# Splitting the gather of the next expert pair's tokens into two parts between the gate and up products of a mixture-of-experts layer

## The chip, the cores and the metric

The kernel runs on one core of one Trainium2 chip. The metric is the device time of one launch in microseconds (us). The kernel before takes 1908.6 us, the median of three runs (1907.25, 1908.6 and 1911.63).

## What is computed

An encoder of two layers over 256 tokens of width 2048, all in float32. Each layer has a mixer (latent attention, dilated attention and an mLSTM, joined by `w_out`) and then a hierarchical mixture of 16 experts of which each token takes two. Only the experts matter for this change. From the reference:

```
def hier_moe(x, wg, bg, we, be, w_gate, w_up, w_down):
    ...
    w = jax.nn.softmax(top_v, axis=-1) * p_grp[..., None]
    eid = grp[..., None] * EXPERTS_PER_GROUP + top_i
    comb = jnp.sum(jax.nn.one_hot(eid, N_EXPERTS, dtype=f32) * w[..., None], axis=-2)
    h = jax.nn.silu(jnp.einsum('bsd,edf->bsef', x, w_gate)) * jnp.einsum('bsd,edf->bsef', x, w_up)
    h = h * comb[..., None].astype(h.dtype)
    return jnp.einsum('bsef,efd->bsd', h, w_down)
```

D_MODEL is 2048 and D_EXPERT 512, so one expert has three weight matrices of 4 MB, and the 16 experts of a layer have 201 MB.

## The kernel before

**The experts in rounds.** The kernel works on two experts at a time, in `NE // 2` = 8 rounds of a layer. An expert has room for CAP = 64 tokens, so a pair fills the 128 columns of the TensorE array: expert 0 of the pair on rows 0 to 63 of the output and expert 1 on rows 64 to 127. The products of the two run side by side on the two halves of the array (form 128*64 in the trace). TensorE executes each float32 matmul of the program as two instructions in the trace.

**One round on TensorE** (lines 1139 to 1175), for the pair i:

- `expert("g0", i)`, `expert("u0", i)`, `expert("g1", i)`, `expert("u1", i)`: gate and up projection, each in two halves of 256 columns. One such call is 32 matmuls of the program (64 in the trace) and reads two loads of weights, one of each expert.
- `turn_h(0, i)` and `turn_h(1, i)` (line 1117): transposes of the gated product, after DVE has multiplied the two halves (line 1816).
- `gather(i + 1)` (lines 1086 to 1096): it picks the tokens of the *next* pair out of `xtok` (in `PR`) by a product with a one-hot matrix `Gm` (in `v_mla`), 4 PSUM banks gx0 to gx3 of 8 matmuls each (32 of the program, 64 in the trace, form 128*128). ScalarE copies the four banks to `XG` (line 2133) once u1 of the present pair is done, since the present pair reads `XG` until then.
- `scatter(i - 1, ...)`: the last pair's result goes back to the tokens; DVE adds it to `X` (line 1787).
- the transposes of line 1159 (weights of the scatter), and then four products dy0 to dy3 with the down projection. They read the loads dn0 (two) and dn1 (two).

**DVE in a round** (lines 1811 to 1834): the product of line 1816 for half 0, the one-hot matrices of the next pair (`tokens_of_pair(i + 1)`, line 1774, stage `gm`) and of the scatter (`gw`), the copy of the transposed half, the same for half 1 with the additions to `X`, and at the round's end the copies of dy1 and dy3 (line 1834).

**The weights.** SyncE's queue (`load`, lines 606 to 610) issues the loads in the order of the list `EXPERT`: for each round g0, g0, u0, u0, g1, g1, u1, u1, dn0, dn0, dn1, dn1. Each is 2 MB. They go round nine places in SBUF (six of `ring`, and `BIAS`, `XN` and `PR`, which are free in this stage). A load waits until the product that read the load nine places before it in the list is done:

```
        def empty(name, l):
...
            if at > 0:
                return ready(LAST_READER.get(before, before), l)
```

Nine of a layer's 96 loads are therefore issued before the first product (they are loads 1 to 9 below), and loads 10 and 11 wait for g0 of round 0, loads 12 and 13 for u0, 14 and 15 for g1, 16 and 17 for u1, 18 and 19 for dy1 of round 0, and so on in the same order through the layer. SyncE works through its waits in order.

**The order of the work** is written out by hand; each engine waits on semaphores: `psum_full` (a bank is written), `psum_free` (a bank is read), `slot_full` (a load has landed) and one for each stage such as `gm`.

Of the kernel before, what the change touches and what calls it, by code (L numbers as in the profile page):

```python
# [52 lines left out]
NE = NG * EPG  # L53
# [312 lines left out]
def build(nc, a, consts, onehot, lncount, out):  # L366
    with ExitStack() as ctx:
# [146 lines left out]
        def after(name, l, j=0, i=None, stride=0):  # L514

            s, n = stages[name]
            return s, l * n + (j + 1) + (0 if i is None else i * stride)
# [9 lines left out]
        def bank(name):  # L527
            return ps[:, BANKS.where(name), :]

        def ready(name, l=0):  # L530

            return psum_full[BANKS.where(name)], BANKS.before(name, l) + 1

        def freed(name, l=0):

            return psum_free[BANKS.where(name)], BANKS.before(name, l)

        def copied(name, l=0):

            return psum_free[BANKS.where(name)], BANKS.before(name, l) + 1  # L540

        def made(name):
            return psum_full[BANKS.where(name)], 1
# [4 lines left out]
        def slot(name):  # L548
            s = SLOTS.where(name)
            return ring[:, s, :] if s < NSLOT else spare[s]  # L550
# [17 lines left out]
        def loaded(name, l):  # L568
            s = SLOTS.where(name)
            return slot_full[s], 16 * (SLOTS.before(name, l) + 1)  # L570
# [131 lines left out]
        def _(pe):  # L702
            def mm(o, lhsT, rhs, start=True, stop=True):
                return pe.matmul(o, lhsT, rhs, start=start, stop=stop, skip_group_check=True)  # L704
# [175 lines left out]
            for l in range(DEPTH):  # L880
# [202 lines left out]
                mm(bank("count")[:, 0:NE], ones[:, :], picked[:, 0, 0:NE], True, False)  # L1083
                mm(bank("count")[:, 0:NE], ones[:, :], picked[:, 1, 0:NE], False, True).then_inc(*made("count"))

                def gather(i):

                    pe.wait_ge(*after("gm", l, i))
                    for n in range(4):
                        name = f"gx{n}_{i}"  # L1090
                        pe.wait_ge(*freed(name, l))
                        for k in range(4):
                            d = (4 * n + k) * P
                            for t in range(NT):
                                last = mm(bank(name)[:, k * 2 * CAP:(k + 1) * 2 * CAP], xtok[:, t, d:d + P], Gm[:, t, :], t == 0, t == NT - 1)
                        last.then_inc(*made(name))

                def expert(n, i):

                    name = f"{n}_{i}"  # L1100
                    w = [slot(f"{n}{j}_{i}").rearrange("p (k c) -> p k c", k=KT) for j in range(2)]
                    for j in range(2):
                        pe.wait_ge(*loaded(f"{n}{j}_{i}", l))
                    pe.wait_ge(*freed(name, l))
                    for k in range(KT):
                        for j in range(2):
                            own_rows = slice(j * CAP, (j + 1) * CAP)
                            last = mm(bank(name)[own_rows, 0:CH], XG[:, k, own_rows], w[j][:, k, :], k == 0, k == KT - 1)
                    last.then_inc(*made(name))

                def turn_h(half, i):

                    name = f"ht{half}_{i}"
                    pe.wait_ge(*copied(f"u{half}_{i}", l))
                    pe.wait_ge(*freed(name, l))
                    for q in range(2):
                        last = pe.transpose(bank(name)[:, q * 2 * CAP:(q + 1) * 2 * CAP], gated[:, (2 * half + q) * P:(2 * half + q + 1) * P], ident)  # L1117
                    last.then_inc(*made(name))

                def scatter(i, ks):  # L1120

                    for k in ks:
                        name = f"sc{k}_{i}"
                        pe.wait_ge(*freed(name, l))
                        for q in range(2):
                            last = mm(bank(name)[:, q * S:(q + 1) * S], Y[:, (2 * k + q) * P:(2 * k + q + 1) * P], Sw)
                        last.then_inc(*made(name))

                def written(i):
                    pe.wait_ge(*copied(f"sw_{i}", l))  # L1130
                    for n in range(4):
                        pe.wait_ge(*copied(f"dy{n}_{i}", l))
# [6 lines left out]
                for i in range(NE // 2):  # L1139
                    for n in range(4):  # L1140
                        pe.wait_ge(*copied(f"gx{n}_{i}", l))
                    expert("g0", i)
                    expert("u0", i)
                    expert("g1", i)
                    turn_h(0, i)
                    if i + 1 < NE // 2:
                        gather(i + 1)
                    expert("u1", i)
                    if i >= 1:
                        written(i - 1)  # L1150
                        scatter(i - 1, range(KT // 4))
                    turn_h(1, i)
                    if i >= 1:
                        scatter(i - 1, range(KT // 4, KT // 2))

                    pe.wait_ge(*freed(f"sw_{i}", l))
                    pe.wait_ge(*after("gw", l, i))
                    for t in range(NT):
                        last = pe.transpose(bank(f"sw_{i}")[0:2 * CAP, t * P:(t + 1) * P], Gw[:, t, :], ident)  # L1159
                    last.then_inc(*made(f"sw_{i}"))  # L1160

                    for half in range(2):
                        pe.wait_ge(*copied(f"ht{half}_{i}", l))
                    for half in range(2):
                        w = [slot(f"dn{half}{j}_{i}").rearrange("p (k c) -> p k c", k=4) for j in range(2)]
                        for j in range(2):
                            pe.wait_ge(*loaded(f"dn{half}{j}_{i}", l))
                        for q in range(2):
                            name = f"dy{2 * half + q}_{i}"
                            pe.wait_ge(*freed(name, l))  # L1170
                            for k in range(4):
                                for j in range(2):
                                    own_rows = slice(j * CAP, (j + 1) * CAP)
                                    last = mm(bank(name)[own_rows, :], hs[:, k, own_rows], w[j][:, k, q * 512:(q + 1) * 512], k == 0, k == 3)
                            last.then_inc(*made(name))
# [3 lines left out]
                with pe.If(due > 0):  # L1179

                    i = NE // 2 - 1
# [87 lines left out]
        def _(dve):  # L1269
# [121 lines left out]
            for l in range(DEPTH):  # L1391
# [385 lines left out]
                def tokens_of_pair(i):  # L1777
                    for j in range(2):
                        ins = one_hot(Gm[:, :, j * CAP:(j + 1) * CAP], 2 * i + j, seen)
                    ins.then_inc(*signal("gm"))  # L1780
# [28 lines left out]
                for n in (1, 3):  # L1809
                    gathered(f"gx{n}_0", n, l)  # L1810
                for i in range(NE // 2):
                    for half in range(2):

                        dve.wait_ge(*copied(f"g{half}_{i}", l))
                        dve.wait_ge(*ready(f"u{half}_{i}", l))
                        dve.tensor_tensor(gated[:, half * CH:(half + 1) * CH], sgs[:, half * CH:(half + 1) * CH],  # L1816
                                          bank(f"u{half}_{i}")[0:2 * CAP, 0:CH], ALU.mult).then_inc(*read(f"u{half}_{i}"))
                        if half == 0:
                            if i + 1 < NE // 2:
                                tokens_of_pair(i + 1)  # L1820
                            for j in range(2):
                                ins = one_hot(Gw[:, :, j * CAP:(j + 1) * CAP], 2 * i + j, comb)
                            ins.then_inc(*signal("gw"))
                        elif i >= 1:
                            add_moe(i - 1, range(KT // 4))
                        dve.wait_ge(*ready(f"ht{half}_{i}", l))
                        dve.tensor_copy(hs[:, 2 * half:2 * half + 2, :].rearrange("p k n -> p (k n)"), bank(f"ht{half}_{i}")[:, 0:4 * CAP]).then_inc(*read(f"ht{half}_{i}"))  # L1827
                    if i >= 1:
                        add_moe(i - 1, range(KT // 4, KT // 2))
                    dve.wait_ge(*ready(f"sw_{i}", l))  # L1830
                    dve.tensor_copy(Sw, bank(f"sw_{i}")[0:2 * CAP, 0:S]).then_inc(*read(f"sw_{i}"))
                    for n in (1, 3):
                        dve.wait_ge(*ready(f"dy{n}_{i}", l))
                        dve.tensor_copy(Y[:, n * 512:(n + 1) * 512], bank(f"dy{n}_{i}")[0:2 * CAP, :]).then_inc(*read(f"dy{n}_{i}"))  # L1834
# [388 lines left out]
```

## Time and profile before

| | |
|---|---|
| median of three runs | 1908.6 us |
| the profiled execution, its own time | 1908.6 us |
| its span, first to last instruction | 1906.8 us |
| PE busy | 1858.8 us (97%) |
| PE weight loads | 1403.1 us (74%) |
| DVE, ACT busy | 624.6 us (33%), 312.2 us (16%) |
| granted TensorE clock, mean | 0.997 of full |
| DMA moved | 544.68 MB, mean 286 GB/s |

The page cuts the span into 40 equal slices of 47.7 us. The experts of layer 0 take about 500 to 952 us, those of layer 1 about 1444 to 1903 us. A row of the chain of waits gives the start of a piece, its length and what ran there; "issue" is time in which the engine waited for nothing that the profile shows. A load's issue is the instruction on SyncE's queue, and "to landing" is the time from there until the last of its 16 parts is in SBUF.

### The profile page before, as it was taken

How to read it: one execution, taken by the hardware profiler on the slowest of the kernel's cores; microseconds unless marked ns; L12 is line 12 of the kernel's file. 1: busy time of each engine (PE TensorE's matmuls, PEld its weight loads, DVE VectorE, ACT ScalarE, POOL GpSimd, SP SyncE). 2: the span in 40 equal slices, each digit the busy share in tenths (PEclk: the TensorE clock that was granted, in tenths of full speed). 3: DMA queues.
4: the chain of work that ended last, by engine and by line, in shares of the span. 5: the costliest groups of instructions: out<-in, count | busy, mean ns of one | idle time of the engine just before them, and what ended most of it. 6: DMA issues, size and time to landing. Idle time of an engine off the chain costs nothing.

```text
span 1906.8 us, 26494 instructions
## 1 busy us (share of the span) xinstructions
PE 1858.8 (97%) x11558; PEld 1403.1 (74%) x11558; DVE 624.6 (33%) x1361; ACT 312.2 (16%) x845; POOL 7.4 (0%) x15
## 2 busy tenths in 40 slices
PE   7999999999999999999999999999999999999998
PEld 7788888788866666656597888877878656666655
DVE  2467664222201221121235675622221121221112
ACT  2122222211211111011021131321111111111010
POOL 0000000000000000000000000000000000000000
PEclk9999999999999999999999999999999999999999
DMA  8342344253699999999694243351647999999995
GB/s 347 141 172 109 156 175 177 96 210 143 273 425 427 426 427 426 428 427 427 287 375 158 113 177 116 150 226 45 246 150 310 425 427 428 427 426 427 428 428 247
DMA packets 40551, 544.68 MB, mean 286 GB/s; under 512 B 4744, under 2 KB 4872, under 8 KB 7792
## 3 DMA queue, kind: packets, MB, share of 16 engines
q1 hardware_dynamic: 38448, 531.46, 67.4%
q0 software_dynamic: 1728, 11.42, 1.5%
q8 instruction: 96, 1.57, 0.3%
q14 instruction: 23, 0.19, 0.0%
q10 hardware_dynamic: 256, 0.04, 0.0%
HBM read 538.69 MB, written 4.22 MB: 285 GB/s over the span
## 4 chain that ended last, share of the span: by engine, by line
PE 95%; DVE 2%; issue 1%; ACT 1%; DMA 1%; SPq 0%; DVEq 0%
PE ps L704 92%; PE ps L758 1%; DMA ring<-in_w_lat 1%; PE ps L1117 1%; ACT prob L1923 0%; PE ps L774 0%; DVE ring L1341 0%; DVE ring L1499 0%; DVE ring L1493 0%; DVE ring L1495 0%; PE ps L766 0%; DVE PR L1580 0%; DVE ss_d L1545 0%; PE ps L1035 0%; PE ps L1159 0%
## 5 line engine op out<-in xcount | busy, mean ns | idle before, releaser
L704 PE MATMUL ps<-ring,scr 128*64 128x256 f32 (+2 forms) x3520 | 559.5, 426 | 7.8 <-issue 7.8
L704 PEld LDWEIGHTS ps<-ring,scr 128*64 128x64 f32 (+1 forms) x3520 | 319.0, 139 | 203.3 <-issue 114.4
L704 PE MATMUL ps<-ring,XN 128*128 128x256 f32 (+2 forms) x1184 | 245.1, 364 | 12.5 <-DMA ring<-in_w_lat 12.5
L704 PEld LDWEIGHTS ps<-ring,XN 128*128 128x128 f32 x1184 | 212.7, 192 | 33.5 <-issue 14.4
L704 PE MATMUL ps<-ring,X 128*128 128x256 f32 x896 | 201.4, 379 | 3.6 <-ACT PR L2002 3.6
L704 PEld LDWEIGHTS ps<-ring,X 128*128 128x128 f32 x896 | 169.8, 190 | 27.3 <-ACT PR L2002 4.4
L704 PE MATMUL ps<-XN,ring 128*128 128x256 f32 x768 | 170.4, 381 | 0.9 <-DVE prob L1303 0.9
L704 PEld LDWEIGHTS ps<-XN,ring 128*128 128x128 f32 x768 | 144.7, 190 | 26.6 <-issue 7.7
L704 PE MATMUL ps<-BIAS,scr 128*64 128x256 f32 (+1 forms) x608 | 157.6, 417 | 6.7 <-issue 6.7
L704 PE MATMUL ps<-PR,scr 128*64 128x256 f32 (+2 forms) x576 | 158.3, 430 | 0.7 <-DVE scr L1827 0.7
L1816 DVE TENSOR_TENSOR v_mla<-scr,ps 128x256 f32<-128x256 f32 x32 | 13.5, 421 | 428.7 <-PE ps L704 428.7
L704 PE MATMUL ps<-XN,scr 128*64 128x256 f32 (+1 forms) x576 | 141.6, 403 | 1.9 <-issue 1.8
L704 PE MATMUL ps<-PR,ring 128*128 128x256 f32 x640 | 142.9, 383 | 0.0
L704 PEld LDWEIGHTS ps<-PR,ring 128*128 128x128 f32 x640 | 121.8, 192 | 19.0 <-issue 2.7
L704 PE MATMUL ps<-PR,prob 128*128 128x256 f32 x512 | 117.0, 382 | 2.3 <-DVE prob L1834 2.3
L704 PE MATMUL ps<-v_mla,PR 128*128 128x128 f32 x1024 | 117.0, 275 | 0.0
L704 PEld LDWEIGHTS ps<-v_mla,PR 128*128 128x128 f32 x1024 | 115.6, 192 | 0.0
L704 PEld LDWEIGHTS ps<-PR,prob 128*128 128x128 f32 x512 | 94.9, 190 | 21.0 <-issue 9.4
L704 PEld LDWEIGHTS ps<-BIAS,scr 128*64 128x64 f32 x608 | 82.9, 138 | 33.3 <-issue 9.7
L704 PEld LDWEIGHTS ps<-PR,scr 128*64 128x64 f32 (+1 forms) x576 | 81.2, 146 | 34.6 <-issue 24.9
L704 PEld LDWEIGHTS ps<-XN,scr 128*64 128x64 f32 x576 | 78.2, 137 | 31.0 <-issue 21.0
L2133 ACT ACTIVATE scr<-ps,par 128x128 f32<-128x128 f32 x240 | 64.0, 413 | 214.4 <-PE ps L704 214.4
(250 smaller groups left out, 1250.6 us busy)
## 6 DMA issues: line engine op xcount, KB each, us to landing
ring<-in_moe_w_up SPq DMA_DIRECT2D x44, 2048.0 KB, 22.9
ring<-in_moe_w_down SPq DMA_DIRECT2D x44, 2048.0 KB, 26.8
ring<-in_moe_w_gate SPq DMA_DIRECT2D x42, 2048.0 KB, 25.0
ring<-in_w_main SPq DMA_DIRECT2D x36, 2048.0 KB, 9.0
ring<-in_w_out_a SPq DMA_DIRECT2D x10, 2048.0 KB, 10.1
PR<-in_moe_w_down SPq DMA_DIRECT2D x10, 2048.0 KB, 24.5
XN<-in_moe_w_gate SPq DMA_DIRECT2D x10, 2048.0 KB, 28.6
BIAS<-in_moe_w_up SPq DMA_DIRECT2D x10, 2048.0 KB, 23.9
```

The source lines that it names most:

```text
L704: return pe.matmul(o, lhsT, rhs, start=start, stop=stop, skip_group_check=True)
L758: last = pe.transpose(bank(name)[:, (kt * NT + t) * P:(kt * NT + t + 1) * P], prob[:, u % 2, j, t, kt * P:(kt + 1) * P], ident)
L1117: last = pe.transpose(bank(name)[:, q * 2 * CAP:(q + 1) * 2 * CAP], gated[:, (2 * half + q) * P:(2 * half + q + 1) * P], ident)
L1816: dve.tensor_tensor(gated[:, half * CH:(half + 1) * CH], sgs[:, half * CH:(half + 1) * CH], bank(f"u{half}_{i}")[0:2 * CAP, 0:CH], ALU.mul ...
L2133: ins = act.activation(XG[:, 4 * n + k, :], bank(name)[:, k * 2 * CAP:(k + 1) * 2 * CAP], ACT.Copy, scale=pcol(l, R_FFN + 4 * n + k))
```

## The change

`gather` takes a list of banks and is called twice in a round, after g0 and after u0, instead of once after `turn_h(0)`. DVE makes the one-hot matrix of the next pair at the start of the round:

```
@@ -1083,10 +1083,10 @@
-                def gather(i):
+                def gather(i, ns=range(4)):
 
                     pe.wait_ge(*after("gm", l, i))
-                    for n in range(4):
+                    for n in ns:
                         name = f"gx{n}_{i}"
                         pe.wait_ge(*freed(name, l))
@@ -1140,11 +1140,13 @@
                     expert("g0", i)
+                    if i + 1 < NE // 2:
+                        gather(i + 1, (0, 1))
                     expert("u0", i)
+                    if i + 1 < NE // 2:
+                        gather(i + 1, (2, 3))
                     expert("g1", i)
                     turn_h(0, i)
-                    if i + 1 < NE // 2:
-                        gather(i + 1)
                     expert("u1", i)
@@ -1809,6 +1811,10 @@
                 for i in range(NE // 2):
+                    if i + 1 < NE // 2:
+                        for n in range(4):
+                            dve.wait_ge(*ready(f"gx{n}_{i}", l))
+                        tokens_of_pair(i + 1)
                     for half in range(2):
@@ -1816,8 +1822,6 @@
                         if half == 0:
-                            if i + 1 < NE // 2:
-                                tokens_of_pair(i + 1)
                             for j in range(2):
```

The number of instructions and of loads stays the same, and so do the banks and the places of the loads.

On PE, round 0 of layer 0, from the last product of g0 to the first of u1, before (`ring,scr` are products of weights, `v_mla,PR` is the gather, L1117 turn_h(0)):

```order
L704 MATMUL ps<-BIAS,scr 64x256
L704 MATMUL ps<-ring,scr 64x256 x65
L1117 MATMUL ps<-K,v_mla 128x128 x2
L704 MATMUL ps<-v_mla,PR 128x128 x32
L704 MATMUL ps<-ring,scr 64x256
```

And the same place with the change:

```order
L704 MATMUL ps<-BIAS,scr 64x256
L704 MATMUL ps<-ring,scr 64x256
L704 MATMUL ps<-v_mla,PR 128x128 x16
L704 MATMUL ps<-ring,scr 64x256 x32
L704 MATMUL ps<-v_mla,PR 128x128 x16
L704 MATMUL ps<-ring,scr 64x256 x32
L1117 MATMUL ps<-K,v_mla 128x128 x2
L704 MATMUL ps<-ring,scr 64x256
```

Half of the gather now stands between g0 and u0 and half between u0 and g1; the transposes of line 1117 are followed by u1 at once.

On DVE, rounds 0 and 1 of layer 0, before (L1774 are the one-hot matrices, eight in a row: four for the next pair, four for the scatter):

```order
L1816 TENSOR_TENSOR v_mla<-scr,ps 128x256 [waits psum_full1,psum_free0]
L1774 TENSOR_SCALAR v_mla<-PR 128x64 x8
L1827 COPY scr<-ps 128x256 [waits psum_full0]
L1816 TENSOR_TENSOR v_mla<-scr,ps 128x256 [waits psum_full3,psum_free2]
L1827 COPY scr<-ps 128x256 [waits psum_full3]
```

With the change (its lines 1776, 1822 and 1831 are lines 1774, 1816 and 1827 of before):

```order
L1776 TENSOR_SCALAR v_mla<-PR 128x64 [waits psum_full6,psum_full7,psum_full5,psum_full4]
L1776 TENSOR_SCALAR v_mla<-PR 128x64 x3
L1822 TENSOR_TENSOR v_mla<-scr,ps 128x256 [waits psum_full1,psum_free0]
L1776 TENSOR_SCALAR v_mla<-PR 128x64 x4
L1831 COPY scr<-ps 128x256 [waits psum_full0]
```

The four for the next pair now stand ahead of the product of half 0 and behind a wait for the four gather banks of the present pair.

## Rows read from the trace of the kernel before

**Rows 1.** The page: DMA share in 40 slices, and what moved
```profile
DMA  8342344253699999999694243351647999999995
GB/s 347 141 172 109 156 175 177 96 210 143 273 425 427 426 427 426 428 427 427 287 375 158 113 177 116 150 226 45 246 150 310 425 427 428 427 426 427 428 428 247
```

**Rows 2.** Chain that ended last, in time order: start, length (us), what
```profile
707.23 0.22 PE ps L1159 x2
...
763.95 0.22 PE ps L1159 x2
...
821.70 0.22 PE ps L1159 x2
...
850.23 2.67 issue
...
883.61 0.22 PE ps L1159 x2
...
919.12 2.29 issue
921.41 12.46 PE ps L704 x80
...
1863.64 2.29 issue
```

**Rows 3.** One issue on SyncE's queue, and its landing: load 92
```profile
L610 SPq DMA_DIRECT2D ring<-in_moe_w_up x1: 328/328/328, 897.8 to 897.8; - x1
DMA to landing us min/median/max: 23.6/23.6/23.6
```

**Rows 4.** Stretches: PE, PEld, DVE, ACT, POOL busy, PEclk, DMA share, GB/s
```profile
500.00:508.00 8.00, 7.95 (x74) 6.43 (x76) 0.00 (x0) 0.38 (x1) 0.00 (x0) 1.00 0.00 0
...
540.00:921.00 381.00, 375.15 (x2779) 245.22 (x2774) 66.76 (x146) 39.23 (x124) 0.00 (x0) 1.00 1.01 427
```

**Rows 5.** Loads 10, 12, 14, 16 and 24: issue on SyncE's queue, landing
```profile
L610 SPq DMA_DIRECT2D BIAS<-in_moe_w_down x1: 328/328/328, 507.2 to 507.2; - x1
DMA to landing us min/median/max: 8.0/8.0/8.0
...
L610 SPq DMA_DIRECT2D ring<-in_moe_w_down x1: 327/327/327, 514.1 to 514.1; - x1
DMA to landing us min/median/max: 11.2/11.2/11.2
...
L610 SPq DMA_DIRECT2D ring<-in_moe_w_gate x1: 327/327/327, 521.0 to 521.0; - x1
DMA to landing us min/median/max: 14.4/14.4/14.4
...
L610 SPq DMA_DIRECT2D ring<-in_moe_w_up x1: 328/328/328, 535.6 to 535.6; - x1
DMA to landing us min/median/max: 10.8/10.8/10.8
...
L610 SPq DMA_DIRECT2D ring<-in_moe_w_down x1: 328/328/328, 565.0 to 565.0; - x1
DMA to landing us min/median/max: 20.5/20.5/20.5
```

**Rows 6.** PE in order of time, round 0: start, length (us), instructions
```profile
520.92 0.44 PE L1117 MATMUL ps<-K,v_mla 128*128 128x128 f32 x2
521.20 7.31 PE L704 MATMUL ps<-v_mla,PR 128*128 128x128 f32 x64
...
527.78 0.72 PE L704 MATMUL ps<-v_mla,PR 128*128 128x128 f32 x5
528.44 0.43 PE L704 MATMUL ps<-ring,scr 128*64 128x256 f32 x1
```

**Rows 7.** DVE in order of time, rounds 0 and 1
```profile
489.30 0.98 DVE L1774 TENSOR_SCALAR v_mla<-PR 128x64 f32<-128x64 f32 x4
...
551.21 0.69 DVE L1834 COPY prob<-ps 128x512 f32<-128x512 f32 x1 [6.17 <-PE ps L704]
```

## The prediction

> **What bounds the kernel now.** I read the page's slices first. From slice 12 to 19 (about 520 to 905 us) and from slice 32 to 39 the 16 DMA engines are full and move 425 to 428 GB/s [rows 1]: the stretches of the experts' weights. PE looks full there too, so the question is which of the two sets the end of a layer. For that I read the chain in order of time. The transposes of line 1159 close each round. From round 3 to round 4 they are 763.95 - 707.23 = 56.72 us apart, with no idle piece on PE. A round reads 12 loads of 2.097 MB. At 427 GB/s [rows 4] one takes 4.91 us, so a round of loads takes 58.9 us. PE is faster than its weights by 2.2 us a round, eats up its lead of nine loads, and then waits: round 5 takes 821.70 - 763.95 = 57.75 us, round 6 takes 61.91 us, and in round 7 PE idles 2.29 us before u1 [rows 2]. That last idle time ends at 921.41 us. Load 92, the second one of u1 in round 7, is issued at 897.8 and lands 23.6 us later, at 921.4 [rows 3]. From there on the work of layer 0 is fixed. Layer 1 does the same: it idles 2.29 us from 1863.64 [rows 2]. So each layer ends a fixed time after its load 92, and the step to cost is what the change does to the line of loads. PE has room of 1.03 + 5.19 + 2.29 = 8.5 us a layer.
>
> The line has no hole. Load 10 lands at 507.2 + 8.0 = 515.2 [rows 5] and load 92 at 921.4: 82 loads in 406.2 us, 4.95 us each. It begins when g0 of round 0 is done, since the DMA engines moved nothing from 500 to 508 us [rows 4]. The change can move load 92 only by moving that start or by making a hole.
>
> **The parts of the change.**
>
> *One-hot matrices earlier on DVE.* In round 0 the four for pair 1 now follow DVE's copies of the first gather, which PE waits for anyway. They take 0.98 us [rows 7] while g0 runs for 6.9 us. In a later round they follow the copy of dy3, which ends at 551.9, so they are done by 552.9 to 553.1. PE wants them after g0 of round 1, about 558. Their new wait for the banks of the present pair is long met, and behind it only the product of half 0 is queued, which waits for u0. Cost 0. If this cover were gone, PE would stand still at the first half of the gather for at most the 0.98 us.
>
> *Banks.* The first half needs gx0 and gx1 free, which are the banks of dy0 and dy1 of the round before. Their copies end within a microsecond of dy1 and dy3, one product before the gather asks. Cost 0. ScalarE's copies to `XG` still wait for u1. Cost 0.
>
> *More changes of form on PE.* Three products of 64 columns (6.92 us each) run from 500.05, and the transposes start at 520.92 [rows 6], so leaving this form costs about 0.1 us. Inside the gather the instructions follow at (527.78 - 521.20) / 59 = 0.1115 us. The last five would end their turns at 528.34, and u1 starts at 528.44 [rows 6]: 0.1 us for coming back. Before, transposes and gather share one such visit. Now there are three visits, two more of 0.2 us: 0.4 us a round, 2.8 us over the seven rounds with a gather. That fits in the room of 8.5 us of the same layer, because the idle time before load 92 only shrinks. Cost 0 while the weights are the bound.
>
> The Trainium skill, "TensorEngine Tiling (Array Packing)", section Key Properties, speaks against the change: changing the tiling mode drains TensorE. It gives no figure. The trace agrees that a change of form costs something, 0.1 us each way here. By the rule with a large drain the sum would be that of the third rival below.
>
> *Places in SBUF free later, in round 0.* This is the term that counts. Half a gather is 32 x 0.1115 + 0.2 = 3.8 us. g0 stays where it is. u0 is done 3.8 us later and g1 7.6 us later. u1 is late by the 0.4 us alone. So load 10 is issued at 507.2 as before, load 12 at 514.1 + 3.8 = 517.9, load 14 at 521.0 + 7.5 = 528.5 and load 16 at 536.0 instead of 535.6 [rows 5]. Loads 10 and 11 are 9.8 us of data. They land at 515.2 and 520.1 to 520.4. A load that finds the engines empty lands 8.0 us after its issue (load 10), of which 4.9 us is data, so the issue must be 3.1 us ahead of the end of the line. At 517.9 it is only some 2.4 us ahead. Two estimates follow.
>
> - Low: load 12 at 517.9 + 8.0 = 525.9 instead of 525.3, load 14 at 528.5 + 8.0 = 536.5 instead of 535.4, so 1.1 us late. Then load 16 may get some back. Before, it is issued at 535.6 with only load 15 in front (about 535.4 + 4.9 = 540.3) and lands at 546.4, 6.1 us after it instead of 4.9. Now it would be issued 5.4 us ahead of load 15's end (541.4) and could land at 546.3. Nothing is lost. If the 6.1 us steps don't appear at loads 12 and 14 at all, up to 1.2 us is won.
> - High: each load that comes with too little in front of it costs a step of 6.1 us, as load 16 did. Load 12 then lands at 526.5 (1.2 us late), load 14 at 537.5 (2.1 us late), and load 16 keeps its own 6.1 us step: 2.1 us late.
>
> I take the high row for loads 12 and 14, being the nearest (load 16 had 4.7 us in front when it was issued, these have less), and give load 16 its step back, since it now has more in front: 2.1 - 1.2 = 0.9, rounded to 1.0 us a layer. Ends: 1.2 us won, 2.1 us lost.
>
> In round 1 the same delay hurts nothing. Load 24 is issued at 565.0 and lands 20.5 us later [rows 5], so 15.6 us of loads are in front of it when it is issued. It can come 3.8 us later, and its successor 7.6 us later. After that PE is faster than the loads and the line in front grows (23.6 us to landing at load 92).
>
> *Idle time of late rounds.* The halves now stand where PE waits for weights, such as the 2.67 us at 850.23 [rows 2], and fill it. PE then reaches u1 of round 6 sooner and waits there or in round 7. Cost 0, gain 0, since load 92 doesn't move.
>
> **Sum.** 2 layers x 1.0 = 2.0 us on the profiled execution's 1908.6 us (its span 1906.8), which is also the median of the runs: 1910.6 us. A difference of 0.2% (3.8 us) is about what a measurement of this kernel can tell from no change, so I forecast no difference that can be told.
>
> **Rivals.**
>
> 1. *The line of loads really runs dry (slower).* The high end holds in both layers, 2 x 2.1 = 4.2 us: 1912.8 us. For it: two pairs of loads are issued within 3.1 us of the end of the line. Against it: load 16 shows that such a step exists before, and the change takes its cause away. It decides above 1.9 us a layer. Chance 0.17.
> 2. *The gather fills real waits (faster).* If PE's own sequence set the end, the idle pieces of rounds 5 and 6 would be saved, of which 2.67 us at 850.23 is the largest; with the 1.03 us of round 5 that is 3.7 us a layer, 7.4 in all: 1901.2 us. For it: the halves stand just where PE waits. Against it: the last wait before u1 of round 7 ends with a landing, 2.29 us after PE is ready. Chance 0.06.
> 3. *PE becomes the bound (slower).* Changes of form cost more than rows 6 show, for instance because two products on the two halves of the array must both finish first. It decides when the two extra visits cost more than 8.5 / 7 = 1.2 us a round in place of 0.4. At 1.6 us it is 11.2 - 8.5 = 2.7 us a layer: 1914.0 us. Chance 0.05.
> 4. *The change doesn't do what it says.* The first half of the gather stands waiting for its one-hot matrix or for a bank, and PE idles in every round. At up to 1 us a round this hides in the room of 8.5 us: 1910.6 us again. Chance 0.03, inside the forecast's number.
>
> **How the numbers follow.** The forecast, with its bounds from -1.2 to just under +1.9 us a layer (1906.2 to 1912.4 us), has 0.69. The chance of slower by over 0.2% is rivals 1 and 3, 0.22. Faster by over 0.2% is rival 2 and a little for a gain nobody sees, 0.07. The rest, 0.71, is within 0.2%. The range reaches from 1906.5, the good end of the landings, to 1914.0, which takes in rivals 1 and 3. It leaves out rival 2.
>
> **What would show it.** Right: in the changed profile the issues in round 0 stand at about 507, 518, 528.5 and 536 us; loads 12 and 14 land about 1 and 2 us later than before, and load 16 about 1 us; DMA moves 427 GB/s from there on; PE's wait before u1 of round 7 ends with load 92 at about 922.4, and rounds 1 to 4 take 57.1 us instead of 56.7. Wrong: rounds above 58 us in a row with no idle piece (rival 3), load 92 at 923.5 or later (rival 1), or u1 of round 7 starting before 921 without a wait (rival 2).

## The result and the profile after

The changed kernel takes 1912.57 us (median of 20 runs, 1909.49 to 1916.98), the one before 1908.2 us (20 runs). The ratio is 1.002, with a 95% interval of 1.0014 to 1.0026: slower by 0.20%, 4.4 us between the medians. The forecast was 1910.6 us in a range of 1906.5 to 1914.0. The profiled execution took 1911.04 us.

The page of the changed kernel, against [rows 1]. The rate in the expert stretches is the same; in layer 0 only the slices in which the stretch begins moved less (259 instead of 273 in slice 11, 416 instead of 425 in slice 12):

```profile
DMA  8343344253699999999794243351646999999995
GB/s 350 147 162 117 148 177 182 88 208 145 259 416 428 427 427 426 428 427 428 303 374 161 109 177 120 145 226 45 264 153 277 429 427 428 427 427 426 427 427 250
```

The chain in order of time, against [rows 2] (start, length in us; line 1161 is line 1159 of before):

```profile
710.92 0.22 PE ps L1161 x2
...
768.33 0.22 PE ps L1161 x2
...
825.74 0.22 PE ps L1161 x2
...
883.15 0.22 PE ps L1161 x2
...
904.16 0.64 issue
...
911.93 2.66 issue
...
922.08 2.29 issue
```

The transposes that close rounds 3 to 6 are all 57.41 us apart, 0.69 us more than the 56.72 of before, and with no idle piece between them. PE doesn't wait in rounds 5 and 6 any more, it waits in round 7, and the last wait is again the one before u1, which ends at 924.37.

Loads 10, 12, 14, 16 and 92 of layer 0, against [rows 5] and [rows 3] (issue on SyncE's queue, then the time to landing):

```profile
L610 SPq DMA_DIRECT2D BIAS<-in_moe_w_down x1: 328/328/328, 508.1 to 508.1; - x1
DMA to landing us min/median/max: 7.8/7.8/7.8
...
L610 SPq DMA_DIRECT2D ring<-in_moe_w_down x1: 328/328/328, 519.0 to 519.0; - x1
DMA to landing us min/median/max: 8.1/8.1/8.1
...
L610 SPq DMA_DIRECT2D ring<-in_moe_w_gate x1: 328/328/328, 529.8 to 529.8; - x1
DMA to landing us min/median/max: 10.7/10.7/10.7
...
L610 SPq DMA_DIRECT2D ring<-in_moe_w_up x1: 328/328/328, 537.2 to 537.2; - x1
DMA to landing us min/median/max: 13.0/13.0/13.0
...
L610 SPq DMA_DIRECT2D ring<-in_moe_w_up x1: 328/328/328, 897.3 to 897.3; - x1
DMA to landing us min/median/max: 27.0/27.0/27.0
```

Everything in this execution is 0.9 us late before the experts begin, so times are counted from load 10's issue. Load 12 is issued 10.9 us after it (6.9 before) and load 14 21.7 us (13.8 before). Load 92 lands 897.3 + 27.0 - 508.1 = 416.2 us after load 10's issue. Before, it is 921.4 - 507.2 = 414.2. Layer 0 thus lost 2.0 us. In layer 1 the same count gives 415.7 against 414.2, 1.5 us lost.

The two profiled spans differ by less than 0.9 + 3.5 us: 1909.26 - 1906.83 = 2.4 us. The other 2.0 us lie between load 92 of layer 0 and g0 of layer 1, 523.2 us before and 521.2 us with the change, and most of them are the clock's. After the wait before u1 of round 7, in which PE is idle for 2.29 us, the granted clock of the kernel before is at 1.2 GHz (0.50) in layer 0, and the next 80 instructions take 12.46 us [rows 2], against 10.78 us in its layer 1 at 2.4 GHz. In the changed kernel the clock stays at 2.4 GHz after the same wait. First the kernel before, then the changed one (the column before the DMA share is the granted clock):

```profile
922.10:925.40 3.30, 3.30 (x18) 2.43 (x16) 0.00 (x0) 0.00 (x0) 0.00 (x0) 0.50 1.02 432
```

```profile
924.50:927.80 3.30, 3.30 (x32) 2.64 (x33) 0.00 (x0) 0.00 (x0) 0.00 (x0) 1.00 0.99 422
```

The clock does not explain the slowdown. Over its 20 executions the changed kernel has a mean granted clock of 0.9970, and the kernel before has 0.9963 to 0.9972 in the three sessions of experiments below. Among executions at 0.998 the changed kernel takes 1911.4 us (mean of 9), the kernel before 1907.0 to 1908.1 us (means of each session, 22 executions).

Where the line of loads lost its time in layer 0 is seen in two stretches of 3 us. The columns are those of [rows 4]; the last one is GB/s. First the kernel before, then the changed one:

```profile
519.50:522.50 3.00, 3.00 (x28) 2.44 (x25) 0.42 (x1) 0.38 (x1) 0.00 (x0) 1.00 0.99 426
530.00:533.00 3.00, 3.00 (x30) 2.00 (x28) 0.00 (x0) 0.00 (x0) 0.00 (x0) 1.00 1.01 431
```

```profile
519.50:522.50 3.00, 3.00 (x29) 3.00 (x27) 0.85 (x4) 0.00 (x0) 0.00 (x0) 1.00 0.87 273
...
530.00:533.00 3.00, 3.00 (x30) 2.02 (x30) 0.42 (x1) 0.18 (x1) 0.00 (x0) 1.00 0.76 262
```

Against 427 GB/s the first stretch lacks (427 - 273) / 427 x 3 = 1.1 us of data and the second one 1.2 us. The first is where load 12 follows loads 10 and 11, the second where load 14 follows 12 and 13.

### The profile page after: what moved, and what is told of

It is laid out like the page before. It is cut to its first block, busy times and chain, and to the rows that moved or that the text cites. A ratio compares the mean times of both kernels' runs of the same rounds, so it can differ in the third digit from the quotient of the medians.

```text
span 1909.3 us, 26536 instructions
## 1 busy us (share of the span) xinstructions
PE 1866.7 (98%) x11558; PEld 1391.0 (73%) x11558; DVE 624.9 (33%) x1361; ACT 312.2 (16%) x845; POOL 7.4 (0%) x15
## 4 chain that ended last, share of the span: by engine, by line
PE 95%; DVE 2%; issue 1%; ACT 1%; DMA 1%; SPq 0%; DVEq 0%
PE ps L704 92%; PE ps L758 1%; DMA ring<-in_w_lat 1%; PE ps L1117 1%; ACT prob L1927 0%; PE ps L774 0%; DVE ring L1343 0%; DVE ring L1501 0%; DVE ring L1497 0%; DVE ring L1495 0%; PE ps L766 0%; DVE PR L1582 0%; DVE ss_d L1547 0%; PE ps L1035 0%; PE ps L1161 0%
## 5 line engine op out<-in xcount | busy, mean ns | idle before, releaser
L704 PEld LDWEIGHTS ps<-ring,scr 128*64 128x64 f32 (+1 forms) x3520 | 306.6, 138 | 203.5 <-issue 107.3
L704 PE MATMUL ps<-v_mla,PR 128*128 128x128 f32 x1024 | 123.7, 280 | 0.0
L1789 DVE TENSOR_TENSOR X<-X,ps 128x512 f32<-128x512 f32 x128 | 88.0, 688 | 27.5 <-PE ps L704 26.7
```

What stands on the lines that cost most here:

```text
L1789: dve.tensor_tensor(x, x, bank(name), ALU.add).then_inc(*read(name))
```

## The experiments

The theory: the line of loads sets the end of a layer, and the two holes in round 0 are the loss. Rivals: the longer rounds (changes of form on PE), the new place of the one-hot matrices on DVE. "In front" of a load means how much later than its issue the load before it lands, and a step is the time from one landing to the next (4.9 us in a full line). Eleven kernels ran. "Load 92" below is its landing counted from the start of g0 in round 0, layers 0 and 1, from one profile. Before it is 421.3 and 421.4; load 10's issue is 7.2 us after g0's start wherever it is left whole. The columns of times are medians against the kernel before on the same chip.

| kernel | load 92 | time, before | ratio (95%) |
|---|---|---|---|
| the change | 423.3, 422.8 | 1912.57, 1908.2 | 1.002 (1.0014 to 1.0026) |
| e1_late_rounds | 421.1, 421.0 | 1908.18, 1907.67 | 1.0006 (0.9997 to 1.0015) |
| e2_round0_only | 423.1, 425.1 | 1912.4, 1907.67 | 1.0033 (1.0022 to 1.0045) |
| e3_dve_only | 420.9, 421.3 | 1908.48, 1907.67 | 1.0009 (1.0 to 1.0018) |
| e11_change_mended | 421.2, 421.1 | 1908.22, 1908.23 | 1.0 (0.999 to 1.001) |
| e6_whole_after_g0 | 425.0, 425.5 | 1918.05, 1908.82 | 1.0047 (1.0034 to 1.006) |
| e8_whole_after_u0 | 422.5, 422.5 | 1912.27, 1908.82 | 1.002 (1.0011 to 1.0029) |
| e9_whole_after_u1 | 420.6, 420.7 | 1906.99, 1908.82 | 0.9987 (0.9979 to 0.9996) |
| e4_early_halves | 420.0, 419.6 | 1906.91, 1907.67 | 0.9994 (0.9985 to 1.0003) |
| e10_halves_after_u1 | 417.9, 418.7 | 1903.74, 1908.82 | 0.9971 (0.996 to 0.9982) |
| e12_pieces_after_u1 | 418.2, 418.2 | 1901.93, 1908.23 | 0.9969 (0.9959 to 0.9978) |
| e13_pieces_split_late | 418.7, 418.0 | 1903.82, 1908.23 | 0.9972 (0.9963 to 0.9982) |

Load 92 and the time do not always move together, and the granted clock is one reason. Four kernels have a lower mean clock than the kernel before on the same chip: e2_round0_only 0.9954 and e4_early_halves 0.9953 against 0.9972, e6_whole_after_g0 0.9942 and e8_whole_after_u0 0.9946 against 0.9963. A straight line through the 24 and the 29 executions of the kernel before on these two chips gives 1.2 and 0.8 us less for each 0.001 more of the clock, so 1.4 to 2.6 us of the time of these four is the clock's, as an estimate. The landings of e4_early_halves promise a gain of 1.3 + 1.8 = 3.1 us and its median gains 0.8; that estimate (1.4 us) covers over half of the difference. At equal clock e2_round0_only still loses the whole amount: its four executions at 0.996 and 0.997 take 1912.0 to 1915.5 us, the twelve of the kernel before at these clocks 1906.2 to 1909.0. Why these four get the lower clock more often is not shown.

### The change cut in two: rounds 1 to 6, and round 0

```
+                    if i + 1 < NE // 2 and i >= 1:
                         gather(i + 1, (0, 1))
...
+                    if i + 1 < NE // 2 and not (i >= 1):
+                        gather(i + 1)
```

In e1_late_rounds the condition is `i >= 1`, in e2_round0_only `i == 0`; `tokens_of_pair(i + 1)` on DVE follows the same condition.

> Round 0 keeps the gather in one piece after the transposes, rounds 1 to 6 have it in two parts. If the loss comes from the line of loads running dry in round 0 (the theory), loads 12, 14 and 16 land as in the kernel before (about 18, 28 and 39 us after the issue of load 10), rounds 1 to 4 take 57.4 us, and the time is that of before within 0.1% (1908 us). If it comes from the longer rounds (rival 1: 0.7 us a round, 6 rounds, 2 layers), it is up to 8 us slower, 1912 us or more. If the loss comes from DVE's order, it stays at about +4 us.

> The other half of the cut: only round 0 has the gather in two parts. Theory: the whole loss of the change, +3 to +4.5 us (1911 to 1912.7), with rounds 1 to 4 at 56.7 us and load 92 some 2 us later counted from load 10's issue. Rival 1 (longer rounds): under +1.5 us. Rival 2 (DVE's order): about +0.6 us, one seventh.

Without the split in round 0 the time is that of before within 0.1%. With the split in round 0 alone the whole loss is there. The rounds of e1_late_rounds are as long as those of the change (line 1163 is line 1159 of before), and still load 92 comes in time, 897.2 + 25.5 - 508.8 = 413.9 us after load 10's issue:

```profile
710.84 0.22 PE ps L1163 x2
...
768.26 0.22 PE ps L1163 x2
```

```profile
L610 SPq DMA_DIRECT2D ring<-in_moe_w_up x1: 328/328/328, 897.2 to 897.2; - x1
DMA to landing us min/median/max: 25.5/25.5/25.5
```

The same two stretches in e2_round0_only show the two holes of the change:

```profile
519.50:522.50 3.00, 3.00 (x29) 3.00 (x29) 1.10 (x5) 0.00 (x0) 0.00 (x0) 1.00 0.83 273
530.00:533.00 3.00, 3.00 (x28) 1.96 (x30) 0.42 (x1) 0.38 (x1) 0.00 (x0) 1.00 0.79 268
```

The lost time varies from layer to layer: 1.8 us in its layer 0 and 3.7 us in its layer 1.

### DVE's part alone

The order on PE is that of before; only `tokens_of_pair(i + 1)` stands at the start of the round.

> Only DVE's part of the change: the one-hot matrix of the next pair at the start of the round, PE's order as before. Theory: 0 within 0.1% (1908 us), rounds 56.7 us. Rival 2 (DVE's order costs): +2 us or more, with PE or DVE waiting where it didn't.

Its interval touches 1.0 and allows up to 0.18%, so the time alone leaves room for a small cost. The landings of load 92 show none.

### The change kept and its line mended

```
+PIECES = {'u0': 2, 'g1': 2}
...
+                        for q in range(n):
+                            for m in (name, PAIRS[name][1]):
+                                sp.wait_ge(*(after(f"{EARLY[m]}_part", l, q) if q < n - 1 else empty(m, l)))
+                                sp.dma_start(slot(m)[:, q * w:(q + 1) * w], source_of(m)[:, q * w:(q + 1) * w]).then_inc(
+                                    early_in[m] if q < n - 1 else slot_full[SLOTS.where(m)], 16)
...
+                        if i == 0 and n in PIECES and k < KT - 1 and (k + 1) % (KT // PIECES[n]) == 0:
+                            last.then_inc(*signal(f"{n}_part"))
```

> The change with all its orders on PE and DVE as they are, and only its line of loads mended: loads 12 to 15 are issued in two halves each, the first when the product that frees the place has read the first 8 of its 16 blocks. The first halves of 12 and 13 go at 14.5 us after g0's start instead of 18.0, those of 14 and 15 at 25.3 instead of 28.8. Theory: load 12 lands at 25.3 and load 14 at 35.3 as in the kernel before, rounds 1 to 4 still take 57.4 us, load 92 is back at 421.3, and the time at 1908 within 1.5 us. If the longer rounds or the changes of form cause the loss, it stays at 1912.

PE and DVE work in the order of the change, and the loss is gone: 1908.22 against 1908.23 us. The two stretches are nearly full again:

```profile
519.50:522.50 3.00, 3.00 (x29) 3.00 (x28) 0.94 (x5) 0.00 (x0) 0.00 (x0) 1.00 0.97 410
...
530.00:533.00 3.00, 3.00 (x30) 1.94 (x30) 0.42 (x1) 0.27 (x1) 0.00 (x0) 1.00 0.99 415
```

This and e1_late_rounds settle the cause, since the longer rounds are all in this kernel too.

### The dose: where the whole gather of round 0 stands

Three kernels move the gather of round 0 as one piece; the other rounds are those of before. In e6 and e8 DVE also makes the one-hot matrix of pair 1 at the start of round 0, as in the change. e6_whole_after_g0:

```
                     expert("g0", i)
+                    if i + 1 < NE // 2 and i == 0:
+                        gather(i + 1)
                     expert("u0", i)
```

e8_whole_after_u0 has the same two lines behind `expert("u0", i)`. e9_whole_after_u1:

```
-                    if i + 1 < NE // 2:
+                    if 1 <= i < NE // 2 - 1:
                         gather(i + 1)
                     expert("u1", i)
+                    if i == 0:
+                        gather(1)
```

> A larger dose, in round 0 only: the whole gather stands between g0 and u0, so u0 and g1 are both about 7.2 us late and u1 is not. Theory: load 12 is issued 21.3 us after g0's start, when loads 10 and 11 have landed (20.4), and lands 8 us after its issue, at 29.3 instead of 25.2; load 14 is 4 to 5 us late, load 16 about 3.6 us. Load 92 is 3 to 4 us later against g0's start in each layer, and the kernel 6 to 8 us slower than before (1914 to 1916). If the split in two (two visits more) were the cause, this kernel, with one visit more, would lose half of what e2_round0_only lost, some 2 us.

> In round 0 only the whole gather stands between u0 and g1. Load 12 keeps its issue, loads 14 and 15 are issued 7.2 us later, at 28.2, about 2 us before load 13 lands. Theory: load 14 lands 8 us after its issue or 6.1 us after load 13, about 1 us late; load 16 is then issued over 5 us before load 15 lands and gets this 1 us back. No loss, within 1 us a layer: 1907 to 1909.5. If every delay of a place costs in proportion, it loses as much as e2_round0_only (the same sum of delays is 3.8 + 7.6 there, 7.2 here): 3 us.

> The opposite direction: in round 0 the gather stands behind u1, so u1 is done 7.2 us earlier and loads 16 and 17 are issued at 28.3 instead of 35.6. Theory: load 16's late step (6.1 us after load 15 instead of 4.9) goes, load 92 is 1.2 us earlier in each layer, and the kernel 2.4 us faster than before, 1905.3. If the time is set by anything but the line of loads, it is as before or slower, since the down products of round 0 now wait longer for the banks.

The largest delay costs most: 3.7 and 4.1 us of load 92, as I had written, and 9.2 us between medians, more than the 6 to 8 that I expected; the lower clock of this kernel is a likely part of it. A loss of 2 us, which would have blamed the number of visits, is excluded. In e6_whole_after_g0 the line is empty for once (load 12 is issued at 522.6):

```profile
520.00:523.00 3.00, 3.00 (x30) 2.01 (x28) 0.34 (x2) 0.00 (x0) 0.00 (x0) 1.00 0.01 5
```

e8_whole_after_u0 went against what I had written. I expected load 14 to be 1 us late and load 16 to make it good. The time is 0.2% longer (partly by the clock, as said), and load 92 is 1.2 and 1.1 us late. Loads 10, 14 and 16 of its layer 0:

```profile
L610 SPq DMA_DIRECT2D BIAS<-in_moe_w_down x1: 328/328/328, 511.4 to 511.4; - x1
DMA to landing us min/median/max: 8.5/8.5/8.5
...
L610 SPq DMA_DIRECT2D ring<-in_moe_w_gate x1: 328/328/328, 532.7 to 532.7; - x1
DMA to landing us min/median/max: 8.4/8.4/8.4
...
L610 SPq DMA_DIRECT2D ring<-in_moe_w_up x1: 328/328/328, 540.1 to 540.1; - x1
DMA to landing us min/median/max: 11.5/11.5/11.5
```

From load 10's issue, load 14 lands at 29.7 (28.2 before, 1.5 late) and load 16 at 40.2 (39.2 before). Load 16 had 5.9 us of loads in front when it was issued, and gave back 0.5 us, not all. e9_whole_after_u1 shows that its late step is only in part a matter of the line. There load 16 is issued 7.2 us sooner, with 11.8 us in front, and still lands 540.4 to 545.8 = 5.4 us after load 15:

```profile
L610 SPq DMA_DIRECT2D ring<-in_moe_w_up x1: 432/432/432, 521.5 to 521.5; - x1
DMA to landing us min/median/max: 18.9/18.9/18.9
...
L610 SPq DMA_DIRECT2D ring<-in_moe_w_up x1: 328/328/328, 528.6 to 528.6; - x1
DMA to landing us min/median/max: 17.2/17.2/17.2
```

Only 0.7 of the 1.2 us by which load 16's step exceeded 4.9 went with the earlier issue (layer 1: 0.5 of 1.0). Load 92 is 0.7 us earlier in each layer, and the kernel 0.13% faster, 1.8 us where I expected 2.4.

### Beginning the line earlier

e4_early_halves issues loads 10 and 11 in halves, the first when g0 has read half of its blocks; e10_halves_after_u1 adds the place of the gather of e9. e12_pieces_after_u1 has `PIECES = {'g0': 4, 'u0': 2, 'g1': 2}` with that place, and e13 adds the split in rounds 1 to 6.

```
+                                for q in range(2):
+                                    for m, (hf, jj) in enumerate(EARLY):
+                                        name = f"dn{hf}{jj}_0"
+                                        sp.wait_ge(*(after("g0_part", l, q) if q < 2 - 1 else empty(name, l)))
...
+                        if name == "g0_0" and k % 8 == 7 and k < KT - 1:
+                            last.then_inc(*signal("g0_part"))
```

> The kernel before, with PE's order kept, but loads 10 and 11 issued in two halves each: the first halves go when g0 of round 0 has read the first 8 of its 16 blocks of columns, 3.5 us before it ends. If the start of the line of loads and nothing else sets the end of a layer, load 92 comes 3.5 us earlier against the start of g0, and the kernel gains 2 x 3.5 = 7 us: 1901 us. If PE's own sequence sets the end (the first rival of the prediction's bound), the time stays at 1908 us. If the shorter transfers of half the size are slower, the gain is below 5 us.

> e4_early_halves with the gather of round 0 behind u1. e4 began the line 3.5 us earlier but load 16, still issued at 35.6, then landed only 1.9 us earlier, 6.7 us after load 15: the line had run low there. With loads 16 and 17 issued at 28.3, load 16 should land at 42.7, 3.7 us earlier than before, and load 92 with it: 2 x 3.7 = 7.4 us faster than before, 1900.3. If the layer's end were bound by PE once the loads are this early, the gain stays near e4's.

> An attempt at a better version: the kernel before with the gather of round 0 behind u1, loads 10 and 11 in four pieces, loads 12 to 15 in two. The first pieces go 1.9 us after g0's start, so the line begins 5.2 us earlier than before (e10: 3.5 us) and never has less than 3 us in front. Theory: load 92 at 421.3 - 4.7 = 416.6, time 1899 to 1901. If pieces of 0.5 MB move slower or the room of PE (5.7 us of idle time in e10) were used up, it stays at e10's 1903.7.

> e12 with the gather in two parts in rounds 1 to 6. With the line begun 5 us earlier, PE has some 4 us of idle time left a layer, and the parts add 0.7 x 6 = 4.2 us of PE time. Theory: the idle time before load 92 is nearly used up, load 92 itself does not move against e12, and the time is 0 to 2 us above e12's. If the two parts had a gain of their own by filling waits, it would be faster than e12.

In e4_early_halves the line began 3.5 us sooner, and load 92 came only 1.3 and 1.8 us sooner, with a ratio that can't be told from 1. Its load 16 is still issued 35.6 us after g0's start, when 2.3 us of loads are in front instead of 4.7, and the line moves 369 GB/s around it:

```profile
541.50:545.50 4.00, 4.00 (x20) 1.61 (x21) 0.09 (x1) 2.94 (x11) 0.00 (x0) 1.00 0.90 369
```

With the gather behind u1 (e10_halves_after_u1) the gain is 5.1 us, where I expected 7.4: load 16 lands 42.6 us after g0's start as forecast, but load 92 is 3.3 and 2.7 us sooner, not 3.7. e12_pieces_after_u1 is the fastest kernel, 1901.93 us, 0.31% below before; e10 is 0.29% below, and the intervals overlap. I expected 1899 to 1901. The line began 5.2 us sooner than before, and load 16 still is 5.3 and 4.7 us sooner (3.7 and 3.6 in e10), but load 92 only 3.1 and 3.2. So by load 16 most of the lead was still there, and it went afterwards; the smaller pieces at the start don't explain it. One place is load 18, which is issued when only 2.7 and 2.8 us are in front and takes steps of 5.7 and 5.4 us. In layer 0 of e12 the line moves 272 GB/s from 507 to 509 us, with little in front of its 0.5 MB pieces, 422 in the 11 us after that, and 369 around the issue of load 18:

```profile
507.00:509.00 2.00, 2.00 (x22) 1.61 (x20) 0.00 (x0) 0.39 (x1) 0.00 (x0) 1.00 0.91 272
509.00:520.00 11.00, 11.00 (x106) 8.76 (x104) 2.21 (x9) 0.00 (x0) 0.00 (x0) 1.00 1.02 422
540.00:546.00 6.00, 6.00 (x30) 2.42 (x28) 0.69 (x1) 0.60 (x1) 0.00 (x0) 1.00 0.96 369
```

Where the rest of the lead went was not followed up. In e13_pieces_split_late the split takes PE's idle time but no gain appears (1903.82 against 1901.93 us, as forecast). In its chain the idle time before g1 of round 7 has shrunk to 0.27 us, against 2.13 us in e12, and load 92 moves by 0.5 and -0.2 us:

```profile
908.94 0.27 issue
...
916.71 2.29 issue
```

The Trainium skill, "DMA: Bandwidth & Descriptors", section Bandwidth, advises transfers of at least 1 MiB for 75% or more of the peak, measured on the GpSimd path. Here, on SyncE's queue, the 1 MB pieces of e11 move 410 and 415 GB/s in the two stretches above, and in e12 the stretch from 509 to 520 us, with pieces of 0.5 MB and 1 MB in a full line, moves 422, 99% of 427.

## Why the prediction was right, and where it was off

- **What bounds a layer.** Right. The wait before u1 of round 7 ends with load 92 in every kernel and in both layers (u1 starts within 0.1 us of the landing). The rest of the layer is of fixed length only at equal clock: from load 92 of layer 1 to the end of the span it is 41.0 us in the kernel before and in the changed one, and 42.7 us in e2_round0_only, where the granted clock is 0.50 from 1873.3 to 1876.6 us, right after that wait.
- **One-hot matrices and banks at 0.** Right as far as the landings go (e3_dve_only).
- **Changes of form** (a visit is leaving the form 128*64 for the gather and coming back). Right that they cost little and are hidden, too small in size. I took 0.2 us a visit and 0.4 us a round from rows 6. A round became 0.69 us longer, 0.35 us a visit. With the half gather the gap between the products of g0 and u0 is 3.9 us, not 3.8:

```profile
508.02 3.84 PE L704 MATMUL ps<-v_mla,PR 128*128 128x128 f32 x32
511.79 1.08 PE L704 MATMUL ps<-ring,scr 128*64 128x256 f32 x8
```

  It stays free because it is hidden: seven rounds cost 4.8 us out of 8.5 us of room. The Trainium skill ("TensorEngine Tiling (Array Packing)", Key Properties) says that such a change drains TensorE. The trace agrees that a visit costs time, but doesn't show what the time is made of, and it is not enough to make PE the bound. Rival 3 needed 1.2 us a round.
- **Places free later in round 0.** The right term, and too small: I took 1.0 us a layer, the profile shows 2.0 and 1.5. From load 10's issue, layer 0 has load 12 at 10.9 + 8.1 = 19.0 us (18.1 before, 0.9 late where I had 1.2), load 14 at 21.7 + 10.7 = 32.4 (28.2 before, 4.1 late, I had 2.1) and load 16 at 42.1 (39.2 before, 2.9 late, I had 0.9). In layer 1 load 14 is 1.7 us late and load 16 1.9 us. Two steps of the working were mis-sized. I gave a load with too little in front a step of 6.1 us, and load 14 of layer 0 took 8.1. And I let load 16 get its late step back: it did in layer 0 (4.9 us), after load 14 had lost twice what I allowed, and did not in layer 1 (6.1 us). The premise of both was that load 16's step of 6.1 us came from its 4.7 us in front. By e9_whole_after_u1 that holds for 0.7 of the 1.2 us above 4.9 in layer 0 and for 0.5 of 1.0 us in layer 1. The two holes of layer 0 are 1.1 and 1.2 us, 2.3 us together, near my high end of 2.1 us a layer.
- **Later rounds.** Right: the same delays in rounds 1 to 6 cost nothing (e1_late_rounds).
- **Sum and rivals.** The time of 1912.57 us lies in the range. But I forecast 2.0 us and no difference that can be told, and that sentence failed: measured were 4.4 us between medians, over twice the sum, just beyond the 3.8 us that I had set as the limit, with an interval (0.14% to 0.26%) that leaves out zero. It is the price of rival 1 (4.2 us) and its mechanism, to which I gave 0.17. The 3.5 us of landings in the one profile lie between the two. My own sign for rival 1, load 92 at 923.5 us or later, is met by the number (924.3) and just missed when the 0.9 us are taken off by which this execution began the experts late (923.4). So the range held partly because it was wide enough to hold the rival. Rival 2 is refuted: the halves do fill waits, the 1.03 and 5.19 us that rounds 5 and 6 took beyond 56.72 [rows 2] are gone, and nothing is gained, since PE waits in round 7 instead. (Not all of it was idle time, as the prediction has it: from 853.9 to 857.2 us the granted clock was 0.50, and 64 instructions took 8.81 us instead of 7.13.) Rival 3 is refuted by e11_change_mended. Rival 4 is refuted by the chain: no idle piece stands in rounds 3 to 6.

## What to carry to other kernels

When a stage is bound by a line of loads, look at the moment at which the line starts. A place in memory freed late there, when little is in front, made a hole that the rest of the line did not make good (2.0 and 1.5 us at load 92), while the same delay in mid-stage cost nothing (e1_late_rounds). Put work that reads no weights behind the products that free places, not ahead of them, in the first round (e9_whole_after_u1: 0.13% faster; ahead of them: up to 0.47% slower), and free a place in parts where the first loads wait for it (e11_change_mended: the whole loss gone; e10_halves_after_u1: 0.29% faster). Work put into idle gaps of an engine that waits for data moves the wait and doesn't shorten it.

## What the runs showed of the hardware beyond this

- A load that follows on a nearly empty line costs a hole though some data is still in front of it: 1.1 us in the change, where load 12 is issued at 519.0 and load 11 lands at 521.6, 2.6 us later. From an empty line a load lands 7.6 us (load 10 of e2_round0_only, layer 0) to 8.9 us (load 12 of e6_whole_after_g0, layer 1) after its issue, of which 4.9 us is data at 427 GB/s. The Trainium skill ("DMA: Bandwidth & Descriptors", Anatomy of one DMA) gives some 2.0 us of fixed cost, for the GpSimd path; the 2.7 to 4.0 us here, on SyncE's queue, are more.
- The hole varies from execution to execution and layer to layer: load 92 was 1.8 us late in one layer of e2_round0_only and 3.7 us in the other, with issues at the same times. Which of the 16 engines is late, and why, stays open.
- Load 16's step of 5.4 us with 11.8 us in front (e9_whole_after_u1) isn't explained by the line running low. It is not alone: in the kernel before, load 44 lands 6.1 us after load 43 with 14.2 us in front, and load 71 lands 6.0 us after load 70 with 27.2 us in front. No run was made on it.
- The wait before u1 of round 7 is followed by a stretch at 1.2 GHz in some executions and not in others. The kernel before has it in layer 0 and not in layer 1, after waits of 2.29 us in both, and pays 12.46 - 10.78 = 1.7 us for it. What decides stays open.
